# A two-layer transformer program on one core: norm, query, scores and expert indices for the first gather made in halves, two loads issued later, convolution taps and GLU banks regrouped, identity matmuls ahead of two waits

## The reference, cut to what matters

```python
def first_block(x, ...):
    h = rmsnorm(x, norm1_g)
    z = h @ w_in + b_in
    glu_val, glu_gate, q, k, v, g_conv, g_attn = split(z)
    u = glu_val * sigmoid(glu_gate)                      # 1024 channels
    y = silu(layernorm(depthwise_conv(u, width 31)))     # per channel, 31 taps
    conv_out = y @ w_conv_out
    attn_out = swa_sink_attention(rope(q), rope(k), v, sinks) @ w_attn_o
    x = x + (sigmoid(g_conv) * conv_out + sigmoid(g_attn) * attn_out) @ w_out
    h2 = rmsnorm(x, norm2_g)
    x = x + peer(h2, w_pq, sub_keys, u_emb, v_emb)
    return rmsnorm(x, final_g)

def peer(h, w_pq, sub_keys, u_emb, v_emb):               # 8 heads, 16 experts each
    q = (h @ w_pq).reshape(B, S, 8, 2, 128)
    sc = einsum("bshcd,hcnd->bshcn", q, sub_keys)        # two sets of 128 scores a head
    s_top, i_top = top_k(sc, 16)
    cand = s_top[..., 0, :, None] + s_top[..., 1, None, :]       # 16 x 16 sums
    best, pos = top_k(cand, 16)
    expert_idx = (i_top[0] * 128 + i_top[1]) at pos
    gate = softmax(best)
    a = gelu(einsum(u_emb[expert_idx], h))               # one dot product per expert
    return sum over experts of gate * a * v_emb[expert_idx]
```

## Time and profile before

| | us |
|---|---|
| median of 3 runs | 1623.15 (1622.27 to 1624.31) |
| the profiled execution | 1624.08 |
| its span, first to last instruction | 1622.2 |
| PE busy | 1448.3 (89% of the span) |
| DVE busy | 989.6 (61%) |
| ACT busy | 621.2 (38%) |
| POOL busy | 317.8 (20%) |
| DMA traffic | 428.55 MB, 264 GB/s in the mean |

### The profile page before, as it was taken

How to read it: one execution, slowest core, us unless ns; L and a number is a source line. 1 busy time by engine, 2 the same in 40 slices (tenths; PEclk the granted TensorE clock), 3 DMA queues, 4 the chain that set the end, 5 groups by cost and what they waited for, 6 DMA issues and landing times.

```text
span 1622.2 us, 16485 instructions
## 1 busy us (share of the span) xinstructions
PE 1448.3 (89%) x5922; PEld 992.2 (61%) x5922; DVE 989.6 (61%) x1967; ACT 621.2 (38%) x1293; POOL 317.8 (20%) x298
## 2 busy tenths in 40 slices
PE   7999999989987777787988769989999999999998
PEld 5868897644542222333333227867888879778886
DVE  3996776667766767776676453236555455565553
ACT  1014572233333333533333224454444335644442
POOL 2000000334534444434435410400000000000000
PEclk9999999999999999999999989999999999999999
DMA  8345653999999999999999964422545443255451
GB/s 318 130 156 149 126 187 119 422 419 415 414 421 420 420 420 420 415 389 417 410 413 419 420 260 157 152 97 104 207 161 202 147 190 142 86 202 187 176 197 62
DMA packets 51777, 428.55 MB, mean 264 GB/s; under 512 B 6648, under 2 KB 6792, under 8 KB 9584
## 3 DMA queue, kind: packets, MB, share of 16 engines
q0 software_dynamic: 40464, 279.18, 43.1%
q1 hardware_dynamic: 11232, 148.33, 24.1%
HBM read 422.49 MB, written 4.98 MB: 264 GB/s over the span
## 4 chain that ended last, share of the span: by engine, by line
PE 65%; DMA 20%; DVE 8%; ACT 4%; issue 2%; POOL 1%; SPq 0%; DVEq 0%; ACTq 0%; POOLq 0%
DMA pool<-uv,experts 19%; PE psum L741 17%; PE psum L1112 11%; PE psum L871 11%; PE psum L872 10%; PE psum L873 10%; PE psum L774 3%; DVE pool L2037 2%; PE psum L818 2%; DMA ring<-stream 1%; DVE ring_lo L1692 1%; ACT diag L1528 1%; ACT xn L1204 1%; POOL pool L699 1%; ACT coef L1522 1%
## 5 line engine op out<-in xcount | busy, mean ns | idle before, releaser
L1112 PE MATMUL psum<-pool,diag 128*128 128x512 f32 x1024 | 477.0, 615 | 119.9 <-ACT diag L1528 119.8
L2037 DVE CUSTOM_DVE_ANT_0 pool<-pool,xn 128x1024 f32<-128x1024 f32 x256 | 313.3, 1225 | 201.0 <-DMA pool<-uv,experts 199.0
L1112 PEld LDWEIGHTS psum<-pool,diag 128*128 128x128 f32 x1024 | 191.8, 194 | 396.2 <-issue 205.6
L699 POOL DMA_INDIRECT pool<-uv,experts x256 | 286.5, 1119 | 505.3 <-PE psum L1112 357.6
L1692 DVE TENSOR_TENSOR ring_lo<-ring,w_hi 128x2048 fp32r<-128x2048 f32 x76 | 173.9, 2292 | 114.0 <-ACT w_hi L1296 114.0
L741 PE MATMUL psum<-hT,ring 128*128 128x256 f32 (+1 forms) x832 | 175.0, 371 | 5.9 <-DMA ring<-stream 4.1
L1518 ACT ACTIVATE acts<-dots 128x2 f32<-128x2 f32 x128 | 26.0, 203 | 379.5 <-DVE dots L2037 379.4
L1296 ACT ACTIVATE w_hi<-ring 128x2048 fp32r<-128x2048 f32 x76 | 144.4, 1908 | 65.5 <-PE psum L873 37.7
L741 PEld LDWEIGHTS psum<-hT,ring 128*128 128x128 f32 x832 | 151.7, 196 | 28.6 <-issue 8.2
L871 PE MATMUL psum<-w_hi,h_hi 128*128 128x512 f32 x400 | 161.3, 403 | 5.1 <-DVE h_lo L1731 4.2
L872 PE MATMUL psum<-ring_lo,h_hi 128*128 128x512 f32 x400 | 157.5, 394 | 0.0
(11 more groups left out here) (267 smaller groups left out, 1858.4 us busy)
## 6 DMA issues: line engine op xcount, KB each, us to landing
ring<-stream SPq DMA_DIRECT2D x66, 2048.0 KB, 7.7
pool<-uv,experts POOLq DMA_INDIRECT x256, 12.7
ring<-stream SPq DMA_DIRECT2D x3, 1024.0 KB, 4.8
t_scratch<-tab POOLq DMA_DIRECT2D x1, 2048.0 KB, 56.8
rpb_scratch<-tab POOLq DMA_DIRECT2D x1, 1792.0 KB, 22.9
ring<-stream SPq DMA_DIRECT2D x1, 1792.0 KB, 6.9
row<-rows POOLq DMA_DIRECT2D x1, 1672.0 KB, 15.5
ring<-stream SPq DMA_DIRECT2D x1, 1664.0 KB, 6.5
```

Of the source, the lines that this page charges most:

```text
L699: gp.indirect_dma_start(out=gath[:, n % NROWS, :], out_offset=None, in_=uv, in_offset=bass.IndirectOffsetOnAxis(ap=experts[:, n:n + 1], ax ...
L1112: last = nc.tensor.matmul(psum[:, RB + half, :], diag[:, n % NDIAG, :], gath[:, n % NROWS, D + 512 * half:D + 512 * half + 512], start=k = ...
L2037: ins = V.tensor_tensor_reduce(out=row_u, in0=row_u, in1=xn[:, n // SLOTS, :], scale=1.0, scalar=0.0, op0=ALU.mult, op1=ALU.add, accum_out ...
```

## The change

- POOL's loads of `row` and `keys` now stand behind the eight small loads of the second table and wait until the second GLU bank is filled.
- The GLU weights are stored in another order, so that one bank holds value and gate of one block of 128 channels. ACT loads the sigmoid's table ahead of the first bank and takes eight sigmoids into a buffer of their own; DVE forms eight products, each followed by taps. Taps go by block: of the blocks whose product is there, the first two unfinished ones take turns. The counts are 13, six times 15 and 84 behind the products, 12 behind the rotation, 4 in each head.
- The root of tile 0 is made from two half squares, with the table loaded ahead of them; the norm is written in two halves and turned in two groups; DVE copies one group, ACT the other.
- The first query's two halves and their two scores are formed one after the other (`first_query_and_scores`), with the first of each in the two sum banks. Half of the products of out (0, 1) stand ahead of tile 0's transposes, the other half behind the first scores, followed by out (1, 1), `tile_query(1, 0)` and `tile_scores(1, 0)`.
- `first_selection` makes expert numbers of the eight best candidates first and signals POOL (`first_ranks`), then of the next eight. Both additions to tile 1's x stand behind it.
- The first four gathers no longer wait for out (1, 1); the fifth does.
- `begin_warm` puts matmuls of the identity with 256 columns of constants into a bank that is overwritten afterwards: 12 ahead of tile 1's `mix0` transposes, 6 ahead of the second layer's first product.

```diff
-TAPS_AFTER_GLU = (28, 31, 31, 80)
+TAPS_AFTER_GLU = (13, 15, 15, 15, 15, 15, 15, 84)
-TAPS_IN_HEAD = 5
+TAPS_IN_HEAD = 4
+ROWS_BELOW_WEIGHTS = 4
+WARM_MIX_NORM, WARM_PAIR = 12, 6
...
-            gp.dma_start(row[:, :], rows.to_broadcast([P, NROW])).then_inc(row_landed, 16)
-            gp.dma_start(keys.rearrange("p m n -> p (m n)"), keys_in).then_inc(keys_landed, 16)
...
             gp.wait_ge(rpb_landed, 16 * HEADS2)
+            gp.wait_ge(bank_filled, FILL_NO["glu", 0, 1] + 1)
+            gp.dma_start(row[:, :], rows.to_broadcast([P, NROW])).then_inc(row_landed, 16)
+            gp.dma_start(keys.rearrange("p m n -> p (m n)"), keys_in).then_inc(keys_landed, 16)
...
-            gp.wait_ge(bank_filled, FILL_NO["wout", 1, 1] + 1)
             for n in range(NT * SLOTS):
-                if n % TOPK == 0:
+                if n == ROWS_BELOW_WEIGHTS:
+                    gp.wait_ge(bank_filled, FILL_NO["wout", 1, 1] + 1)
+                if n == 0:
+                    gp.wait_ge(first_ranks, 1)
+                elif n == TOPK // 2:
+                    gp.wait_ge(selected, 1)
+                elif n % TOPK == 0:
                     gp.wait_ge(selected, n // TOPK + 1)
...
+            def begin_warm(name, count):
+                dst = begin(name)
+                for _ in range(count):
+                    nc.tensor.matmul(dst[:, 0:S], ident, cst[:, 0:S], start=True, stop=True)
+                return dst
...
+                dst = begin_warm(first + (0,), WARM_PAIR) if layer == 1 and q == 0 else begin(first + (0,))
                 pe.wait_ge(h_split, split_before + 2)
-                tile_products(first, layer, q, halves, 0)
+                tile_products(first, layer, q, halves, 0, dst)
...
-            tile_transposes("mix0", 1, xn[:, 1, :])
+            tile_transposes("mix0", 1, xn[:, 1, :], WARM_MIX_NORM)
...
+            nc.scalar.activation(unused, eps, ACT.Sigmoid)
+            for m in range(KD):
+                b = wait_filled(act, ("glu", m // 2, m % 2))
+                nc.scalar.activation(glu_sig[:, m, :], b[:, S:2 * S], ACT.Sigmoid, bias=par_("b_glu")[:, KD + m:KD + m + 1]
+                                     ).then_inc(sigmoid_ready, 1)
...
+            def first_root():
+                load_roots()
+                wait_emptied(act, ("wout", 0, 0))
+                step(nc.scalar.activation(xn[:, 0, 0:512], x[:, 0, 0:512], ACT.Square, accum_out=ssq_half[:, 0:1]))
+                step(nc.scalar.activation(half_bias, ssq_half[:, 0:1], ACT.Identity, bias=eps, scale=1.0 / D))
+                wait_emptied(act, ("wout", 1, 0))
+                step(nc.scalar.activation(xn[:, 0, 512:D], x[:, 0, 512:D], ACT.Square, accum_out=ssq_half[:, 1:2]))
+                nc.scalar.activation(rstd[:, 0:1], ssq_half[:, 1:2], ACT.Sqrt, bias=half_bias, scale=1.0 / D
+                                     ).then_inc(root_ready, 1)
...
+                ranks(0).then_inc(first_ranks, 1)
+                link(V.match_replace(first_cand, best[:, 0:8], first_cand, -3.0e38))
+                ranks(8).then_inc(selected, 1)
...
             add_tile(1, 0)
-            second_norm(0)
+            first_norm()
+            first_selection()
             add_tile(0, 1)
-            for k in range(SELECT_STEPS):
-                select_step(0, k)
             add_tile(1, 1)
```

188 lines of the change are left out of this document (136 added, 52 removed).

## The result

The changed kernel takes 1615.78 us (median of 5 runs, 1614.63 to 1616.65) against 1624.31 for the kernel before on the same chip (1622.27 to 1627.95): a ratio of 0.9942, 95% interval 0.9928 to 0.9955, faster by some 8.5 us. Timed once more, in the experiments, the ratio was 0.9917 (0.9901 to 0.9933). One of those six executions ran at a granted clock of 0.56 in the mean and took 2447.96 us; medians and ratios are of the other five. The profiled execution has a span of 1614.0 us, 8.2 less than the span of 1622.2 before. The forecast was 1613.5, in a range of 1609.5 to 1618.0.

The account below looks back on a forecast made before the run. Head bound by PE and its waits, gather stage by bytes once running, tail by PE. Terms -4.1 + 0 - 2.9 - 3.0 + 0 = -10.0 us gave 1614.1 or 1613.2; 1613.5 was taken, range 1609.5 to 1618.0.

Parts of the forecast that it names:

- the slow stretch: Start of the GLU: PE's first matmuls run at half pace again, as long as before; 3.0 us allowed before DVE's first product.
- Part 1: Head: with row and keys loaded later, the first weight chunk lands before PE is free, so PE starts sooner; -4.1 us.
- Part 2: Head: smaller GLU banks and reordered taps leave DVE just in time, with PE as cover; 0 us.
- Part 3: Chain to the first gather: first gather issued 6.9 us earlier, but the gather stage gains only 2.9 us.
- The ring: Query chunk loads ahead of the gathers, released by output products: full DMA flow begins 4 us sooner.
- a dip of more than 2 us near 307: Gather stage: a DMA share dip this long around the ninth gather would show the prediction wrong.
- Rival (a): Early gather stage stays on PE, tile 1's chain holding later gathers too; gather gain only 0.6, time 1616.4; chance 0.14.
- Part 4: Behind the gather stage: twelve identity matmuls keep the clock up for tile 1's transposes and the projections; -3.0 us.
- Part 5: Second layer's first product: six identity matmuls just fit PE's 2.80 us wait, where the clock stayed up; 0 us.
- Rival (b): Tile 1's last transposes: clock falls in spite of the twelve identity matmuls, worth 0; time 1617.1; chance 0.10.
- (c): Head: first weight chunk still lands late, three chunks sharing one queue; late loads worth 1 us, time 1617.2; chance 0.07.
- (e): Both identity matmul places: they meet a slow clock and overrun their gaps; slower, 1625.9 or 1629.0; chance 0.03.

Follow-up runs that it names:

- Kernel 1: Kernel before with only the row and keys loads issued later, behind the second filled GLU bank; 1620.33 us, ratio 0.9968.
- 2: Changed kernel without the twelve identity matmuls ahead of tile 1's transposes behind the gather stage; 1617.54 us, ratio 0.9949.
- 8: Changed kernel without the six identity matmuls ahead of the second layer's first product; 1615.77 us, ratio 0.9922.
- 9: The changed kernel run again as it is, beside three others on one chip; 1612.96 us, ratio 0.9917.
- 6: Kernel 5 with seven identity matmuls added ahead of tile 1's transposes, in front of the ninth gather; 1620.27 us, ratio 0.9962.
- 7: Kernel 4 with tile 1's root ahead of the copy of tile 0's second score, and four identity matmuls instead of seven; 1614.32 us, ratio 0.9920.
- 12: Kernel 7 with seven more identity matmuls ahead of the second attention's first query transposes; 1611.99 us, ratio 0.9918.
- 10: Kernel 7 with the first eight gathers waiting for all sixteen ranks, first gather about 4 us later; 1615.24 us, ratio 0.9928.
- Kernel 4: Changed kernel with seven identity matmuls ahead of tile 1's transposes, before the ninth gather; 1616.34 us, ratio 0.9944.
- Kernel 5: Kernel before with only the late loads and the twelve identity matmuls ahead of tile 1's mix0 transposes; 1618.78 us, ratio 0.9953.
- kernel 11: Kernel 5 with the six identity matmuls ahead of the second layer's first product added; 1617.00 us, ratio 0.9938.
- 3: Changed kernel with the first eight gathers waiting for all sixteen ranks of the first selection; 1616.52 us, ratio 0.9944.

## Why the prediction was right, and where it was not

The time lies inside the range, 2.3 us above the forecast, and in part by luck: the head gained 2.0 us more than forecast, the gather stage 2.0 less, and 2.2 were given back in the tail. The landmarks came nearly all where it had put them: PE's start 13.8 (13.1), the wait ahead of the bias sum 0.64 (0.4), transposes 1.09 (1.04) at a clock of 1.00. DVE's first product came at 21.5 and not at 23.5, since the slow stretch that was allowed 3.0 us did not come. Allowing for the head's extra 2.0 us, first gather, ninth gather and the take of the eighth row came within 0.5 us (269.71, 301.25 and 304.54, forecast 272, 303.2 and near 306). The last dot product stands at 948.9, forecast 949, and that is two errors of 2.0 us that cancel.

- **Part 1, -4.1: mis-sized.** The start was right to 0.7 us. That PE would be the later one was not: the chunk landed at 13.7 and not at 12.0, so PE still waited for it, 0.99 us here and 0.26 to 1.25 in eleven of the twelve kernels. I had named that wait as a sign that I was wrong; it costs less than 1 us. The step "I take as long a slow stretch again" failed by more: PE's stretch was 2.8 us shorter in nine of 13 executions, 1.1 to 1.5 in four. Kernel 1 shows that the loads alone bring it: -6.85. Why the slow stretch shrank is open. The wait of 4.1 us is there in one profile only, and among the 13 a shorter wait didn't go with the full pace: three of the four slower ones waited 0.3 us or less.
- **Part 2, 0: right.** DVE's first product at 21.52 instead of 29.47 (kernel 1) moved nothing.
- **Part 3, -2.9: the step that failed.** Four profiles of this stage give 695.67, 696.63, 694.73 and 695.75 (kernels after, 2, 8 and 9), in the mean 0.9 less than 696.58; that difference lies within the scatter of the stage lengths, so what follows rests on the bytes moved and not on it. The ring, the gathers and tile 1's chain moved as worked out. What failed is "one us after the DMA engines ran dry ... later gathers are bound by bytes". They had drained the first eight rows by 301, as the lead of the ring (4.3 us by the bytes) was larger than that of the buffers (0.5); they lost 2.6 us between 301 and 313 while each gather waited for PE to sum a row. I had named a dip of more than 2 us near 307 as a sign that I was wrong; it is there. Half of the lead that was left at 75 us (0.8 MB, 1.9 us) was gone at the end. Rival (a), with 0.14, is nearest: 0.6 for 0.9.
- **The two limits.** Before, bytes and PE's chain through tile 1 ended nearly together, as far as these runs show. PE's chain alone shortened (6) gives 0, the ring and first gather alone (the change) 0.9, both (7 and 12, and 10 without the early first gather) 2.9 to 4.0 against the kernel before. Kernel 4 had both as well and kept 0.3: a low clock at the next query took its lead. Which part of part 3 brings the bytes is half settled: not the early ranks (10), and so most likely the cut order on PE that releases the ring; the ring's release wasn't tried alone.
- **Part 4, -3.0: right,** 2.7 in the first pair, 3.5 in the second. Left out was that a clock held up here may fall later: of the 2.2 us given back in the tail, the 1.7 near 1030 are of that kind. Five of eleven against none of three is too few to call it a cause.
- **Part 5, 0: right for the profile of before, not for the changed kernel.** There the clock had stayed up in a wait of 2.80 us; in all four executions with late loads and without the six it fell in it or within 2 us behind it. Kernel 5 shows the wait and a PEclk of 0.69 behind it, and kernel 11 the 0.8 us. The Trainium skill (TensorE: Matmul & The Clock Gate, "HAM oscillation — how this bites in real kernels") tells of waits in which the clock falls, but the waits that it describes are longer than these 2.80 us, so its words did not say that the six would pay here, as the prediction took from them.

Rival (a), by the same count, gives 1616.4, which is nearer to the measured 1615.8 than the sum's 1614.1. Rival (b) occurred once in eleven profiles, in part (11). Of (c) the late landing came, by 1.7 us, but not its price; (e) did not occur.

## What to carry to other kernels

Where buffers are refilled as they are used up, a lead at the first transfer is worth only what the first *re-use* gains too: find what the ninth of eight buffers waits for, and count the bytes moved by a fixed point of the stage (24.0, 24.8, 25.8 MB here) rather than the time of the first issue. Count again behind the next point at which PE is late: kernel 4 had 25.8 MB too, and lost its lead at the next query. When one execution shows the clock up in a wait of nearly 3 us, price the case in which it isn't: in four of five profiles without the six it was down at the same wait. And take a late load out of the start before anything cleverer: here two moved lines brought 5 of 8.5 us.

## What the runs showed of the hardware

The granted clock of the same code changed from execution to execution: over the 80 matmuls near 1030 us the changed kernel had it low for 3.4 us in one profile and about 10 in the other. Its cost, 0.8 to 5 us a place, is as large as most edits of this change. Identity matmuls held it up in each of the four places where they were put (twelve before 961, six before 1315, seven before 278, seven before 1055), with one partial miss, at 0.44 to 0.46 us each (24 records in 5.34 us for twelve, 14 in 3.19 for seven). By the traces a low clock also cost bytes, where row sums release the buffers of the gathers: with one right ahead of a query the DMA engines moved 96 and 147 GB/s for 4 us (kernels 3 and 4; 276 at the lowest in the changed kernel, whose clock was low for half as long).
